# The loop over expert pairs on TensorE, written out in straight line

## What is computed

```python
gate, idx = lax.top_k(aff.transpose(0, 2, 1), cap)
xs = jax.vmap(lambda hb, ib: hb[ib])(h, idx)
a = jnp.einsum('becd,edf->becf', xs, w1)
b = jnp.einsum('becd,edf->becf', xs, w3)
y = jnp.einsum('becf,efd->becd', jax.nn.silu(a) * b, w2) * gate[..., None].astype(h.dtype)
```

## Time and profile before

| what | value |
|---|---|
| time, median of 3 runs | 3372.94 us (3371.18 to 3386.62) |
| the profiled execution's own time | 3376.32 us |
| its span, first to last instruction | 3374.6 us |
| PE busy | 2892.1 us, 86% of the span |
| PE weight loads busy | 2129.3 us, 63% |
| DVE, ACT, POOL busy | 867.7, 492.4, 237.5 us |
| mean granted TensorE clock | 0.944 |
| DMA: mean rate | 181 GB/s |
| weight loads in the expert stages | 192 of 2048 KB, 10.3 us each from issue to landing (median, two or three at a time) |

### The profile page before, as it was taken

How to read it: one execution, slowest core, us unless ns; L and a number is a source line. 1 busy time by engine, 2 the same in 40 slices (tenths; PEclk the granted TensorE clock), 3 DMA queues, 4 the chain that set the end, 5 groups by cost and what they waited for, 6 DMA issues and landing times.

```text
span 3374.6 us, 70152 instructions
## 1 busy us (share of the span) xinstructions
PE 2892.1 (86%) x32580; PEld 2129.3 (63%) x32580; DVE 867.7 (26%) x1443; ACT 492.4 (15%) x862; POOL 237.5 (7%) x254
## 2 busy tenths in 40 slices
PE   6999999999958777778589999999999577777784
PEld 3555666666638777778445456666565477777783
DVE  4943222331140000000169322233211400000003
ACT  2011033330020000000020111333200200000001
POOL 0320000000000000000005000000000000000000
PEclk9999999999979998899899999999999798999897
DMA  7222202102119888889652221101111398888894
GB/s 295 104 113 104 98 30 80 53 26 106 75 64 340 323 328 319 311 325 361 263 215 100 106 101 69 74 30 53 52 80 75 119 354 326 318 318 317 321 356 148
DMA packets 55211, 611.66 MB, mean 181 GB/s; under 512 B 6256, under 2 KB 6256, under 8 KB 20720
## 3 DMA queue, kind: packets, MB, share of 16 engines
q1 hardware_dynamic: 38736, 550.52, 42.3%
q0 software_dynamic: 7168, 24.12, 2.9%
q10 hardware_dynamic: 8992, 32.11, 2.5%
HBM read 576.84 MB, written 29.88 MB: 180 GB/s over the span
## 4 chain that ended last, share of the span: by engine, by line
PE 76%; issue 9%; DVE 8%; DMA 6%; ACT 1%; POOL 0%; SPq 0%; POOLq 0%; DVEq 0%; ACTq 0%
PE ps L279 65%; DVE region_b L1033 4%; DMA ring<-in_w_exp 2%; PE ps L522 2%; DMA ring<-in_w_mix 2%; PE ps L649 1%; PE ps L495 1%; PE ps L505 1%; PE ps L576 1%; PE ps L559 1%; DVE rstd L990 0%; DMA ffn_rows<-region_b,rstd 0%; DMA region_x<-ffn_rows 0%; DVE rstd L982 0%; PE ps L434 0%
## 5 line engine op out<-in xcount | busy, mean ns | idle before, releaser
L279 PE MATMUL ps<-region_r,ring 128*64 128x80 f32 x24192 | 960.4, 242 | 266.9 <-issue 256.0
L279 PEld LDWEIGHTS ps<-region_r,ring 128*64 128x64 f32 x24192 | 926.4, 144 | 301.5 <-issue 295.1
L279 PE MATMUL ps<-hT,ring 128*128 128x320 f32 (+2 forms) x3600 | 1021.9, 442 | 18.8 <-DVE region_b L1021 9.6
L279 PEld LDWEIGHTS ps<-hT,ring 128*128 128x128 f32 x3600 | 611.8, 192 | 379.9 <-issue 234.1
L279 PE MATMUL ps<-region_b,ring 128*128 128x320 f32 (+2 forms) x896 | 259.2, 441 | 3.6 <-DMA ring<-in_w_mix 3.6
L1033 DVE SCALAR_TENSOR_TENSOR region_b<-region_b,params 128x655 f32<-128x655 f32 x240 | 243.9, 1016 | 8.5
L1219 DVE TENSOR_TENSOR region_r<-ps,region_r 128x320 f32<-128x320 f32 x64 | 31.5, 491 | 828.2 <-PE ps L680 828.2
L279 PEld LDWEIGHTS ps<-region_b,ring 128*128 128x128 f32 x896 | 160.2, 192 | 76.4 <-issue 24.5
L954 ACT ACTIVATE region_r<-ps 128x320 f32<-128x320 f32 x64 | 28.0, 438 | 1143.3 <-PE ps L680 1143.3
L279 PE MATMUL ps<-region_x,ring 128*128 128x512 f32 (+1 forms) x480 | 139.4, 449 | 3.7 <-DVE region_x L1159 3.7
L1224 DVE COPY region_r<-ps 128x320 f32<-128x320 f32 x64 | 31.5, 492 | 358.4 <-PE ps L680 358.4
(11 more groups left out here) (193 smaller groups left out, 2014.0 us busy)
## 6 DMA issues: line engine op xcount, KB each, us to landing
ring<-in_w_exp SPq DMA_DIRECT2D x192, 2048.0 KB, 10.3
ring<-in_w_mix SPq DMA_DIRECT2D x68, 2048.0 KB, 11.4
x_store<-region_m ACTq DMA_DIRECT2D x2, 2560.0 KB, 12.3
ffn_rows<-region_r ACTq DMA_DIRECT2D x4, 1280.0 KB, 18.4
region_m<-x_store ACTq DMA_DIRECT2D x2, 2560.0 KB, 10.4
h_rows<-region_x ACTq DMA_DIRECT2D x10, 512.0 KB, 2.7
region_x<-ffn_rows ACTq DMA_DIRECT2D x4, 1280.0 KB, 9.3
rstd<-in_bias POOLq DMA_DIRECT2D x16, 192.0 KB, 2.7
```

The source lines that it names most:

```text
L279: ins = pe.matmul(*args, **kw)
```

## The change

The hardware loop goes. A Python loop calls `expert_pair` with a plain number for each of the eight pairs, so the instructions of all sixteen experts stand one after the other in TensorE's program, and there are eight copies of the pair's code instead of three. Where `q` was a register it is a constant; the slot waits still depend on the layer's register. The order of the matmuls, the waits and the work of all other engines are the same, and so are SyncE's loop over the pairs and the loops over the layers.

```diff
--- before.py
+++ after.py
@@ -708,10 +708,8 @@
                             expert_block(q, n + 4 + half, y_ps[:, half, 0:4 * CAP], act, "y_done")
 
                 turn_rows(0)
-                expert_pair(0, True, False)
-                with pe.Fori(1, EPAIRS - 1) as q:
-                    expert_pair(q, False, False)
-                expert_pair(EPAIRS - 1, False, True)
+                for q in range(EPAIRS):
+                    expert_pair(q, q == 0, q == EPAIRS - 1)
                 turn_y(NE - 1)
 
                 for k in range(KC):
```

## The result

The changed kernel takes **3303.46 us** (median of 4 runs, 3288.18 to 3306.48) against 3379.78 us for the kernel before in the same series (4 runs, 3371.18 to 3391.5). The ratio is 0.9761, 95% interval 0.9734 to 0.9787. The forecast was 3301 us. The profiled execution took 3302.70 us, 73.6 us less than the profiled execution of before; the forecast was 72.6 us less.

A forecast was written before the change was run, and what follows sets the result against it. TensorE with its waits for instruction packets was taken to bound the kernel, weight loads close behind. Terms of -64.9 and -7.7 us sum to -72.6, from the 3372.9 us median to 3301 us; range 3270 to 3336.

The forecast's parts named there:

- Term 1: Expert stages: removing ten taken loop branches removes ten joints, TensorE pauses of 5.6 to 7.1 us between pairs: -64.9 us.
- Rival 3: Pair loop's branch only covers a wait ending at the same time, which returns in the same places: 3373 us; 3%.
- Term 2: Inside expert pairs: pairs 2 to 6 at 76 us each gain 10.7, pair 7 at 75 us loses 3.0: -7.7 us.
- The base: Whole kernel before the change: median of the runs 3372.9 us, from which the forecast time was reckoned.
- second stop: Two matmuls after a jump TensorE stops again, 2.56 us; target near its packet's end, so one jump waits for two packets.
- Apart from the part of one that each jump threw away: TensorE's instruction queue: as many packets fetched as before, except the part of one discarded at each jump.
- A pair can't come much under 71.4 us: Expert pairs: weight loads, close behind TensorE, set a floor of 71.4 us, from 26.4 MB at 370 GB/s.
- Rival 2: Expert stages: fetches and loads take part back, pairs run at 79.4 us, 29.6 us gained: 3343 us; 15%.

The follow-up runs named there:

- without jump: Changed kernel with pairs 1 to 6 each in a one-pass loop, so register waits and branches return but no branch is taken: 3301.98 us.
- near jumps: Changed kernel with a six-pass loop over one already met wait ahead of pairs 2 to 6, 50 taken jumps in all: 3301.03 us.
- moved target: Kernel before with already met waits ahead of its pair loop, moving the jump's target within its packet: 3368.28 us with 12 waits, 3351.94 us with 24.
- straight kernel: The changed kernel, pair loop written out, against the kernel before: 3303.46 us, and 3297.64 us when run again.
- long pause: Straight kernel with a 20-pass loop over one already met wait ahead of pairs 2 to 6: 3360.84 us.
- light loads: An eighth of each block of expert weights loaded: 3115.47 us for the kernel before with its loop, 3015.72 us for the straight kernel.
- one wide group: Straight kernel with one of four column groups in matmuls of 128 columns instead of two of 64: 3230.22 us; with the pair loop back, 3327.46 us.
- all four groups wide: Straight kernel with all four column groups of each expert block in matmuls of 128 columns instead of two of 64: 3612.55 us.

## Why the prediction was right

**Term 1** (-64.9 us, the ten joints) was right and is shown: nine are gone, in the tenth place stands a weight wait of 2.92 us, so -62.0. (The same program run again has none there but 0.8 us in another of the ten: such waits change from one execution to the next.) The runs without jump, with near jumps and with a moved target say why: it is the fetch of a far target, not the branch, the registers or a hidden wait. Rival 3 is refuted. "Advanced Engine Details and Errata" of the Trainium skill, section "Control Flow Timing", has about 108 ns for a compare-and-branch; the runs show 74 to 95 ns not taken, 214 ns taken to a near target, and up to 7.4 us to a far one. "Runtime: NRT & Kernel Launch" of the Trainium skill, section "Instruction fetch mechanics", says that a taken branch must wait for a fetch if its target isn't in the window of blocks held; the runs agree.

**Term 2** (-7.7 us) came out near in sum, but by errors that cancel. Pairs 2 to 6 gained 4.3 us and not 10.7 (I took 76 us for each; they took 76.6 on average). Pair 7 gained 3.6 us where I had it lose 3.0 because its packets' ends would lie elsewhere. No cause can be read off that: in the second trace of the same program, with the same positions, it gained 1.0. Pairs 0 and 1 were to stay and moved by 2.4 and -1.1 us over both layers. That makes -68.6 us; the stages lost 70.8, since the first matmuls of a pair now overlap the last ones of the pair before by 0.2 us at each joint. Single pairs spread from 70.4 to 81.0 us, wider than the 74 to 78 that I named, and one stop of 3.19 us was above my 3. The stages came at 602.6 and 605.7 us, against some 606 and 608. But those forecasts start from the hand-set stretches of the earlier trace rows, 4 us longer than from first to last matmul; like for like some 602 and 604 were forecast. The clock came at 0.97 and 0.95. That term 2 came so near is luck: its two parts were off by 6.4 and 6.6 us in opposite directions, and the stages of the straight kernel's two traces differ by 3.5 us.

**The base** was low. The prediction starts from a median of 3372.9 us; the kernel before has 3379.8 with its fourth run and 3379.7 to 3382.4 in the later series. The gain by medians is 76 to 84 us and not 72.6. That both were low by some 7 us lets them cancel in the 3301, which is luck too.

**The reasoning behind term 2** is not borne out. I took the stock of weights in the slots for what the jump gave back. The long pause fills them just as well, and is given back only 0.7 us of 6.7. And the second stop is not free: behind the ten jumps it takes 23.6 us, and 24 to 28 us were gained when the moved head took it away. Yet the pairs that held it were only 0.4 us longer each than in straight line. So a pair behind a jump with full loads gets one or two microseconds back from somewhere: a jump costs 7.4 to 8.4 us there, and 9 to 10 where TensorE is busy from end to end, with light loads or one wide group. That it comes out of waits for packets and loads is argued from these prices, and no run separates them.

**Packets.** "Apart from the part of one that each jump threw away" was too little: it was 2.7 packets a jump. And the 246 instructions a packet divide the instructions of all engines by the packets of TensorE's queue alone; with 256, as the wide runs show, the 252 to 256 between stops fit better than I had it.

**"A pair can't come much under 71.4 us"** was wrong: one pair of the changed kernel took 70.4 us at 371 GB/s, and it is 69.2 us with one wide group, at 388 GB/s and a DMA share of 1.01. I had scaled a rate of 348 GB/s by its share of 0.94; the rate at full share is higher than that.

**Rival 2** (loads and packets take part back) names the right next limit, as the runs with light loads and with fewer instructions show, but the pairs had been paying for it before the change already.

## What to carry to other kernels

A hardware loop with a body of thousands of instructions pays for each jump back: 7 to 10 us here. The duration of the branch itself shows most of it, and 2 to 3 us of it can be only for where the loop's head lies in a packet. Write such loops out, or make a pass longer. From what distance on a jump costs a fetch was not measured: the near target lay a few instructions away, the others 3100, 6200 and a whole layer, and the branches to the last two took 3.4 to 5.9 us, no longer than those to the first. Where an engine of many short instructions stops at regular counts with nothing to release it, count its instructions: beside full weight loads fewer and longer ones won 70 us here, although they cost the engine more busy time.

## What had not been expected of the hardware

Weight loads hold up the packets of instructions: with an eighth of the weights the stops at packets' ends were gone, but for those right behind a jump. "Mostly hidden", as the Trainium skill says of the crossing between blocks of instructions ("Runtime: NRT & Kernel Launch", "Instruction fetch mechanics"), is true of the straight kernel with light loads (a pair takes 57.5 us and PE is busy for all of it) and not of the one with full loads.

In the kernel with all four groups wide, TensorE worked at the lower of its two clock levels, 1.2 GHz, for about 100 us without a pause, and only then at 2.4 GHz; in the kernel before, pair 0 of layer 0 had 0.97 of the clock, 0.57 in its first 4.4 us and 1.00 in the 8 behind them. Busy time by stretch: up to 1120 us, from there to the end of pair 0, pair 1:

```profile
1008.13:1120.00 111.87, 111.87 (x582) 111.71 (x583) 3.34 (x7) 3.86 (x6) 2.46 (x3) 0.56 0.44 155
1120.00:1143.61 23.61, 23.51 (x214) 23.35 (x214) 1.86 (x4) 0.44 (x1) 0.93 (x1) 1.00 0.84 303
1143.45:1232.80 89.35, 89.15 (x804) 88.84 (x804) 5.69 (x12) 4.27 (x8) 4.69 (x4) 1.00 0.85 298
```

The engine was busy for all of the 111.87 us and granted 0.56 of its clock: 0.88 of them at half, 98 us, and the rest at full. Cut finer, every stretch up to 1105 us has 0.50 and the one from 1110 us on has 1.00. Before it lay the same waits as in the kernel before (the last one 1.12 us in both), and the first matmuls were of 128 columns of weights instead of 64. In layer 1 pair 0 took 135.0 us too. Why it took so long to rise is open; no run was made on it.
